# Interleaving the last sixteen adaLN modulation blocks with the first mixer tile

## The chip, the cores and the metric

The kernel runs on all 8 cores of one Trainium2 chip. Each core computes one element of the batch (4096 rows of 1024) with the same program; nothing is exchanged. The metric is the device time in microseconds of the slowest core.

## The reference

A hybrid decoder layer: adaLN modulation from a conditioning vector, a mixer (chunked gMLP gating beside multi-scale pooling), and a squared-ReLU MLP.

```python
mod = jax.nn.silu(c) @ w_ada + b_ada            # 1024 -> 6144, one row per core
shift1, scale1, gate1, shift2, scale2, gate2 = [
    m[:, None, :] for m in jnp.split(mod, N_MOD, axis=-1)]
h = rms_norm(x, norm1_pre) * (1.0 + scale1) + shift1
z = h @ w_in
y_a = spatial_gating(z[..., : 2 * D_A], ...)    # gelu, layer norm, 128x128 mixing
y_b = multiscale_pool(z[..., 2 * D_A:], ...)    # windows 2, 4, 8, 16
mix = jnp.concatenate([y_a, y_b], axis=-1) @ w_out
x = x + gate1 * rms_norm(mix, norm1_post)
h = rms_norm(x, norm2_pre) * (1.0 + scale2) + shift2
f = jnp.square(jax.nn.relu(h @ w_fc1)) @ w_fc2  # 1024 -> 4096 -> 1024
x = x + gate2 * rms_norm(f, norm2_post)
```

## The kernel before

The rows are worked in 16 tiles of 256. Weights w_in, w_out and w_fc1 stay in SBUF as bf16; their loads are issued on POOL's queue because they cast from float32 ("casts" below: w_out one of 4 MB read, w_fc1 four of 4 MB read). w_fc2 streams through three slab slots; in ffn(0) each slab is cast by a POOL DMA and written back to HBM by SP, later tiles read that copy.

Every engine runs its instructions in the order in which the program records them (`sc.op`, `sc.dma`); semaphore waits follow from the buffers named as read and written. A buffer that is overwritten waits for its readers.

*Modulation (L233 to L288).* w_ada is taken in 24 blocks of 256 columns, 1 MB each. A block b goes: SP loads it into staging slot b % 3 of `xb` (L237, needs the slot's last reader, L257, done) and a bias row into `rl` (L239, needs the matmul of block b-2 done). ScalarE multiplies by silu(c) in eight instructions (L250). VectorE adds up in three (L253, L255, L257), TensorE sums over the partitions (L261, L262, which also mark `modgate b`), VectorE copies the row out (L265). Then either TensorE turns the row into columns of PSUM bank 0 (L285; chunks 0, 1, 3, 4, here "plain" blocks), or, for the gates gate1 (blocks 8 to 11) and gate2 (blocks 20 to 23), TensorE broadcasts it (L273) and VectorE multiplies it into gp1 or gp2 (L276; here "gate" blocks). L298 to L302 then make the scale columns.

*Large weights.* POOL issues the cast of w_out after `modgate8` (L289), those of w_fc1 after `modgate12`, 16, 20 and 23 (L293). Every fc1 matmul (L616) names all four w_fc1 buffers as read.

*mixer(i)* is a generator. Between its yields stand these steps: norm_A (squares on ScalarE, then a chain of eight small VectorE instructions, L178 to L190); an empty one; norm_A2 (L346, L348); norm_B (transposes L359, scaling L368 on ScalarE and L377 on VectorE); z (L407, L412); u and v with pooling 0 and 1 and the layer norm (L450 to L487); pooling 2 and 3 (L426, L430); the spatial matmuls (L501, L509, L514); the pooling matmuls (L525, L534); the first and the second half of the output matmuls with the residual (L548 to L567), a step each; an empty one; norm_A, norm_A2, norm_B of the second norm. Tile 0's input sits in slot 0 of `xb`, which is also a staging slot.

*ffn(i)* runs fc1 and fc2 (L616, L635) over 16 pairs of hidden blocks; from its second step on it takes one step of mixer(i+1) after each of its own. mixer(0) has no ffn to stand beside and runs alone after block 23 (L686).

Of the kernel before, what the change touches and what calls it, by code (L numbers as in the profile page):

```python
# [78 lines left out]
def build(NT=16):  # L79
# [21 lines left out]
    sc = Sched()  # L101
# [3 lines left out]
    with contextlib.ExitStack() as _st:  # L105
# [32 lines left out]
        def buf(name):  # L138
            if name not in B:
                B[name] = Buf(name)  # L140
            return B[name]
# [88 lines left out]

        wada_v = wada_d.rearrange("p (b k c) -> p b k c", b=24, k=8)
        CH_COL = {0: 0, 1: 8, 3: 16, 4: 24}
        for b in range(24):  # L233
            st = b % 3
            stg = xb[:, st, :].rearrange("p (k c) -> p k c", c=256)
            stg_bufs = [buf("xb%d_0" % st), buf("xb%d_1" % st)]
            sc.dma(SP, lambda e, b=b, stg=stg: e.dma_start(out=stg, in_=wada_v[:, b, :, :]),  # L237
                   "wa%d" % (b % 3), writes=stg_bufs)
            sc.dma(SP, lambda e, b=b: e.dma_start(out=rl[0:1, b % 2, 0:256], in_=bada_d[0:1, b * 256:(b + 1) * 256]),  # L239
                   "ba%d" % (b % 2), writes=[buf("rl%d" % (b % 2))])  # L240
            pr = 4 + b % 2
# [13 lines left out]
            sc.op(DVE, lambda e, stg=stg: e.tensor_tensor(out=stg[:, 0:2, :], in0=stg[:, 0:2, :], in1=stg[:, 2:4, :],  # L255
                                                          op=ALU.add), reads=stg_bufs, writes=stg_bufs)
            sc.op(DVE, lambda e, stg=stg, accv=accv: e.tensor_tensor(out=accv, in0=stg[:, 0, :], in1=stg[:, 1, :],  # L257
                                                                     op=ALU.add), reads=stg_bufs, writes=[mb_])

            def mm_mod(e, b=b, pr=pr, accv=accv):  # L260
                e.matmul(ps[0:1, pr, 0:256], lhsT=ones[:, 0:1], rhs=accv, start=True, stop=False)  # L261
                return e.matmul(ps[0:1, pr, 0:256], lhsT=ones[0:1, 0:1], rhs=rl[0:1, b % 2, 0:256], start=False, stop=True)  # L262
            sc.op(PE, mm_mod, reads=[buf("macc%d" % (b % 2)), buf("ones"), buf("rl%d" % (b % 2))],
                  writes=[Bps(pr), buf("modgate%d" % b)])
            sc.op(DVE, lambda e, b=b, pr=pr: e.tensor_copy(out=tmp[0:1, b % 2, 0:256], in_=ps[0:1, pr, 0:256]),  # L265
                  reads=[Bps(pr)], writes=[buf("tmp%d" % (b % 2))])
            chunk = b // 4
            if chunk in (2, 5):
                gp = gp1 if chunk == 2 else gp2
                gpb = buf("gp1") if chunk == 2 else buf("gp2")  # L270
                pb = 6 + b % 2
                cols = slice((b % 4) * 256, (b % 4) * 256 + 256)
                sc.op(PE, lambda e, b=b, pb=pb: e.matmul(ps[:, pb, 0:256], lhsT=ones[0:1, :], rhs=tmp[0:1, b % 2, 0:256],  # L273
                                                        start=True, stop=True),
                      reads=[buf("tmp%d" % (b % 2)), buf("ones")], writes=[Bps(pb)])
                sc.op(DVE, lambda e, gp=gp, pb=pb, cols=cols: e.tensor_tensor(out=gp[:, cols], in0=ps[:, pb, 0:256],  # L276
                                                                          in1=gp[:, cols], op=ALU.mult),
                      reads=[Bps(pb), gpb], writes=[gpb])
            else:
                col0 = CH_COL[chunk] + (b % 4) * 2  # L280

                def mm_col(e, b=b, col0=col0):
                    ins = None
                    for q in range(2):
                        ins = e.matmul(ps[:, 0, col0 + q:col0 + q + 1], lhsT=tmp[0:1, b % 2, q * 128:(q + 1) * 128],  # L285
                                       rhs=ones[0:1, 0:1], start=True, stop=True)
                    return ins
                sc.op(PE, mm_col, reads=[buf("tmp%d" % (b % 2)), buf("ones")], writes=[Bps(0)])  # L288
        sc.dma(POOL, lambda e: e.dma_start(out=w_out_sb[:], in_=wout_d.rearrange("p (k n) -> p k n", k=8)),  # L289
               "w_out", reads=[buf("modgate8")], writes=[buf("w_out")])  # L290
        fc1_v = fc1_d.rearrange("p (k n) -> p k n", k=8)
        for q in range(4):
            sc.dma(POOL, lambda e, q=q: e.dma_start(out=fc1_sb[:, 2 * q:2 * q + 2, :], in_=fc1_v[:, 2 * q:2 * q + 2, :]),  # L293
                   "fc1_%d" % q, reads=[buf("modgate%d" % (12 + 4 * q if q < 3 else 23))], writes=[buf("fc1_%d" % q)])
        FC1 = [buf("fc1_%d" % q) for q in range(4)]

        x_load(0)
        sc.op(DVE, lambda e: e.tensor_copy(out=mc[:, 0:32], in_=ps[:, 0, 0:32]), reads=[Bps(0)], writes=[buf("mc_raw")])  # L298
        sc.op(DVE, lambda e: e.scalar_tensor_tensor(out=mc[:, 32:40], in0=mc[:, 8:16], scalar=1.0,
                                                    in1=cv[:, C_N1:C_N1 + 8], op0=ALU.add, op1=ALU.mult),  # L300
              reads=[buf("mc_raw"), buf("cv")], writes=[buf("mc_g1")])
        sc.op(DVE, lambda e: e.scalar_tensor_tensor(out=mc[:, 40:48], in0=mc[:, 24:32], scalar=1.0,  # L302
                                                    in1=cv[:, C_N2:C_N2 + 8], op0=ALU.add, op1=ALU.mult),
              reads=[buf("mc_raw"), buf("cv")], writes=[buf("mc_g2")])
        MODB = [buf("mc_raw"), buf("mc_g1"), buf("mc_g2")]
        G1, SH1, G2, SH2 = 32, 0, 40, 16

        sc.op(DVE, lambda e: e.tensor_tensor(out=vg[:, 0, :], in0=vg[:, 0, :], in1=vg[:, 1, :], op=ALU.mult),
# [40 lines left out]
                                                 op0=ALU.mult),  # L349
                  reads=[buf("xb%d_1" % slot), r_buf], writes=[buf("hbf_1")])  # L350

        def norm_B(dstT, dstT_buf, gcol, shcol):
            for s in range(2):
                mb = MB[s]

# [28 lines left out]
        def mixer(i):  # L384
# [6 lines left out]
            yield  # L391
            norm_A2(slot, r1, br1)
            yield
            norm_B(hT, "hP%d" % (i % 2), G1, SH1)
            yield
            if i > 0:
                sc.op(DVE, lambda e: e.tensor_copy(out=Z[:, :, 0:16], in_=Z[:, :, 256:272]),
# [176 lines left out]
            yield  # L574
            norm_A2(slot, r2, br2)
            yield
            norm_B(hT, "hP%d" % (i % 2), G2, SH2)
            yield

        def slab_load(G):  # L580
# [100 lines left out]
            yield  # L681

        stores = []
        if NT > 1:
            x_load(1)
        for _ in mixer(0):  # L686
            pass
        for i in range(NT):
            gm = mixer(i + 1) if i + 1 < NT else None
            step = 0  # L690
# [109 lines left out]
```

How the kernel before makes its waits and increments, by code:

```python
            def run(eng_name, eng):  # L715
                waited = {}
                for (deps, fn, key, amt) in sc.ops[eng_name]:
                    for (k_, v_) in deps:
                        if waited.get(k_, 0) >= v_:
                            continue
                        eng.wait_ge(sems[k_], v_)
                        waited[k_] = v_
                    if fn is None:
                        continue
                    ins = fn(eng)
                    ins.then_inc(sems[key], amt)
```

## Time and profile before

| | us |
|---|---|
| median of two runs | 1629.02 (1625.27 to 1632.77) |
| profiled execution, its own time | 1626.7 |
| its span, slowest core (core 4) | 1624.9 |
| spans of the eight cores | 1608.6 to 1624.9 |
| mean granted TensorE clock, die 0 and die 1 | 0.961, 0.958 |

All rows are of core 4. Times are microseconds from the start of the span. A timeline row reads: start, duration, engine, line, operation, output<-input with sizes, count of instructions merged, and in brackets the engine's idle time ahead of it and what ended it. PE is TensorE, DVE VectorE, ACT ScalarE, SPq the sequencer of SyncE that issues DMAs. A windows row gives a stretch, its length, for each engine the busy time and number of instructions (PE, PE's weight loads, DVE, ACT, POOL), the granted TensorE clock as a share of full speed, the mean busy share of the 16 DMA engines, and GB/s.

### The profile page before, as it was taken

To read this page: it belongs to the slowest core of one execution; us is meant where nothing else is said; L and a number is where in the kernel's file an instruction comes from. 1 tells how busy PE (TensorE), PEld (TensorE's weight loads), DVE (VectorE), ACT (ScalarE), POOL (GpSimd) and SP (SyncE) were. 2 spreads that over 40 slices of the span, in tenths; PEclk is the share of its full clock that TensorE was granted. 3 is DMA by queue.
4 is the path that set the end of the run, shared out by engine and by line. 5 is a ranking of instruction groups with operands and counts; after the bars stand their busy time and mean duration, and the time that the engine had idled before them with its cause. 6 is when DMAs were issued, how large, how long until landed. Compare 5 with 4: busy or idle time off the path is not lost.

```text
span 1624.9 us, 27071 instructions; the slowest of 8 cores (1608.6 to 1624.9 us)
## 1 busy us (share of the span) xinstructions
PE 1331.5 (82%) x8674; PEld 855.0 (53%) x8818; DVE 767.3 (47%) x1993; ACT 595.6 (37%) x1315; POOL 326.2 (20%) x319
## 2 busy tenths in 40 slices
PE   0543345989898989898989898989899898999896
PEld 0211023647565656565656565656566565656564
DVE  0443344445555454554546364645454545464531
ACT  1544323334342524242525242434343342424231
POOL 0000001322222122221222122222122222122221
PEclk9999987999999999999999999999999999999998
DMA  8478823994342424242524233343433342433243
GB/s 205 181 201 196 225 51 79 207 188 145 104 146 94 156 92 169 78 169 78 182 74 150 102 121 127 104 156 104 156 103 138 107 140 99 157 100 135 91 157 117
DMA packets 88491, 218.79 MB, mean 135 GB/s; under 512 B 5768, under 2 KB 5920, under 8 KB 84384
## 3 DMA queue, kind: packets, MB, share of 16 engines
q1 hardware_dynamic: 82704, 194.87, 35.0%
q0 software_dynamic: 5648, 22.19, 8.7%
q8 instruction: 73, 1.20, 0.3%
q14 instruction: 66, 0.54, 0.1%
HBM read 214.05 MB, written 25.17 MB: 147 GB/s over the span
## 4 chain that ended last, share of the span: by engine, by line
PE 54%; DVE 23%; DMA 11%; issue 6%; ACT 3%; POOL 1%; DVEq 1%; SPq 1%; ACTq 0%; POOLq 0%
PE ps L635 18%; PE ps L616 15%; PE ps L548 7%; DMA fc2buf<-fc2s 5%; DMA xb<-wada 5%; DVE pt L426 4%; PE ps L407 4%; PE ps L450 3%; PE ps L465 3%; DVE xb L673 3%; DVE tmpS L509 2%; DVE sm L187 2%; DVE xb L253 1%; DVE tmp L661 1%; DVE vg L661 1%
## 5 line engine op out<-in xcount | busy, mean ns | idle before, releaser
L616 PE MATMUL ps<-hP,fc_sb 128*128 128x256 bf16 x4096 | 510.4, 281 | 7.2 <-ACT rl L620 4.4
L635 PE MATMUL ps<-fc2buf,hid 128*128 128x512 bf16 x1936 | 474.7, 385 | 29.3 <-DMA fc2buf<-fc2s 13.8
L616 PEld LDWEIGHTS ps<-hP,fc_sb 128*128 128x128 bf16 x4096 | 410.2, 101 | 103.1 <-issue 11.7
L622 POOL TENSOR_TENSOR hid<-rl 128x512 bf16<-128x512 f32 x256 | 272.7, 1067 | 936.2 <-ACT rl L620 872.4
L635 PEld LDWEIGHTS ps<-fc2buf,hid 128*128 128x128 bf16 x2048 | 201.5, 100 | 226.3 <-issue 42.0
L620 ACT ACTIVATE rl<-ps 128x512 f32<-128x512 f32 x256 | 152.1, 595 | 421.1 <-PE ps L616 413.6
L261 PE MATMUL ps<-rl,ones_sb 128*1 128x256 f32 x48 | 24.3, 609 | 114.7 <-DVE rl L257 112.7
L548 PE MATMUL ps<-w_out_sb,yT 128*128 128x512 bf16 x496 | 116.4, 383 | 2.3 <-DVE yT L534 1.4
L250 ACT ACTIVATE xb<-xb,sm 128x256 f32<-128x256 f32 x192 | 78.4, 493 | 106.8 <-DMA xb<-wada 106.8
L368 ACT ACTIVATE hP<-ps,mc 128x128 bf16<-128x128 bf16 x256 | 92.7, 467 | 29.8 <-PE ps L359 29.8
L377 DVE TENSOR_SCALAR hP<-ps,mc 128x128 bf16<-128x128 bf16 x256 | 67.5, 337 | 73.5 <-PE ps L359 73.5
L552 ACT ACTIVATE junk<-ps 128x512 bf16<-128x512 f32 x64 | 38.2, 597 | 147.6 <-PE ps L548 143.3
L548 PEld LDWEIGHTS ps<-w_out_sb,yT 128*128 128x128 bf16 x512 | 50.3, 99 | 63.4 <-issue 4.6
L558 DVE TENSOR_TENSOR tmp<-ps,gp 128x512 f32<-128x512 f32 x32 | 22.1, 692 | 126.0 <-ACT junk L552 126.0
L426 DVE TENSOR_TENSOR pt<-Z 128x271 f32<-128x271 f32 x64 | 28.2, 440 | 106.8 <-ACT Z L412 103.3
L346 ACT ACTIVATE hbf<-xb,sm 128x1024 bf16<-128x1024 f32 x32 | 36.7, 1148 | 96.1 <-DVE sm L190 96.1
L340 ACT ACTIVATE junk<-xb 128x1024 bf16<-128x1024 f32 x64 | 67.4, 1053 | 8.3 <-DVE xb L567 5.2
L525 PE MATMUL ps<-diff,wpool_sb 128*128 128x256 bf16 x64 | 14.6, 317 | 65.9 <-DVE tmpS L509 65.9
L261 PEld LDWEIGHTS ps<-rl,ones_sb 128*1 128x1 f32 x48 | 2.7, 80 | 120.4 <-issue 120.4
L514 POOL TENSOR_TENSOR yT<-tmpS,ubf 128x512 bf16<-128x512 f32 x32 | 36.9, 1152 | 139.2 <-DVE tmpS L509 139.2
L187 DVE SCALAR_TENSOR_TENSOR sm<-sm 128x2 f32<-128x2 f32 (+1 forms) x192 | 54.8, 285 | 20.7 <-DVE sm L185 0.3
L661 DVE TENSOR_TENSOR tmp<-ps,gp 128x512 f32<-128x512 f32 x32 | 22.1, 692 | 89.5 <-ACT junk L655 88.1
(80 smaller groups left out, 1238.3 us busy)
## 6 DMA issues: line engine op xcount, KB each, us to landing
fc2buf<-fc2s SPq DMA_DIRECT2D x240, 512.0 KB, 3.8
xb<-wada SPq DMA_DIRECT2D x24, 1024.0 KB, 7.7
xb<-x SPq DMA_DIRECT2D x16, 1024.0 KB, 6.1
out<-xb SPq DMA_DIRECT2D x16, 1024.0 KB, 5.0
fc_sb<-w_fc POOLq DMA_DIRECT2D x4, 2048.0 KB, 19.9
fc2buf<-w_fc POOLq DMA_DIRECT2D x16, 512.0 KB, 7.8
fc2s<-fc2buf SPq DMA_DIRECT2D x16, 512.0 KB, 6.3
w_in_sb<-w_in POOLq DMA_DIRECT2D x2, 1536.0 KB, 23.4
```

What stands on the lines that cost most here:

```text
L187: sc.op(DVE, lambda e: e.scalar_tensor_tensor(out=u, in0=t, scalar=-0.5, in1=vv, op0=ALU.mult, op1=ALU.mult), reads=[bt_, bv], writes=[bu])
L250: ins = e.activation(out=stg[:, k, :], in_=stg[:, k, :], func=AF.Identity, scale=scv[:, k:k + 1])
L340: sc.op(ACT, lambda e, s=s: e.activation(out=junk[:], in_=xs(slot, s), func=AF.Square, accum_out=sm[:, ss_col + s:ss_col + s + 1]), reads= ...
L368: ins = e.activation(out=dstT[:, k, s * 128:(s + 1) * 128], in_=bank_bf(mb)[:, k * 128:(k + 1) * 128], func=AF.Identity, scale=mc[:, gcol ...
L377: ins = e.tensor_scalar(out=dstT[:, k, s * 128:(s + 1) * 128], in0=bank_bf(mb)[:, k * 128:(k + 1) * 128], scalar1=mc[:, gcol + k:gcol + k ...
L407: ins = e.matmul(ps[:, mb, gg * T:(gg + 1) * T], lhsT=w_in_sb[:, k, 1024 + g * 128:1024 + (g + 1) * 128], rhs=hT[:, k, :], start=(k == 0), ...
L426: sc.op(DVE, lambda e, src=src, dst=dst, lo=lo, sh=sh: e.tensor_tensor(out=dst[:, lo:272], in0=src[:, lo:272], in1=src[:, lo - sh:272 - sh ...
L548: ins = e.matmul(ps[:, mb, :], lhsT=yT[:, k, s * 128:(s + 1) * 128], rhs=w_out_sb[:, k, hf * 512:(hf + 1) * 512], start=(k == 0), stop=(k ...
L616: ins = e.matmul(ps[:, fb, jj * T:(jj + 1) * T], lhsT=fc1_sb[:, k, j * 128:(j + 1) * 128], rhs=h2T[:, k, :], start=(k == 0), stop=(k == 7))
L620: sc.op(ACT, lambda e: e.activation(out=rl[:, jp % 2, :], in_=ps[:, fb, :], func=AF.Relu), reads=[Bps(fb)], writes=[buf("rl%d" % (jp % 2))])
L622: sc.op(POOL, lambda e: e.tensor_tensor(out=hid[:, jp % 3, :], in0=rl[:, jp % 2, :], in1=rl[:, jp % 2, :], op=ALU.mult), reads=[buf("rl%d" ...
L635: ins = e.matmul(ps[:, 2 * s + hf, :], lhsT=hid[:, jp % 3, jj * T + s * 128:jj * T + (s + 1) * 128], rhs=fc2buf[:, sl, jj, hf * 512:(hf + ...
```

## The change

The modulation block becomes a function `mod_block(b)`. Blocks 0 to 7 run as before on three staging slots. Then the scale and shift of the first norm are made (`mod_cols(1)`), tile 0 is loaded into slot 0 and mixer(0) is begun: after each of the blocks 8 to 23 the generator takes one step. These blocks have two staging slots, 1 and 2. The gate broadcast moves from PSUM banks 6 and 7, which the mixer uses, to 2 and 3. The columns of the second norm are made after block 19. The large casts are issued behind the blocks that gate them (`late_weights`), since POOL's queue now also holds instructions of mixer(0). L308 to L318 (the spatial weights) now stand ahead of block 0 instead of behind block 23.

```diff
-        for b in range(24):
-            st = b % 3
+        def mod_block(b):
+            st = b % 3 if b < 8 else 1 + b % 2
...
-                   "wa%d" % (b % 3), writes=stg_bufs)
+                   "wa%d" % st, writes=stg_bufs)
...
-                pb = 6 + b % 2
+                pb = 2 + b % 2
...
+        def late_weights(b):
+            if b == 8:
+                sc.dma(POOL, lambda e: e.dma_start(out=w_out_sb[:], in_=wout_d.rearrange("p (k n) -> p k n", k=8)),
+                       "w_out", reads=[buf("modgate8")], writes=[buf("w_out")])
+            for q in range(4):
+                if b == (12 + 4 * q if q < 3 else 23):
+                    sc.dma(POOL, lambda e, q=q: e.dma_start(out=fc1_sb[:, 2 * q:2 * q + 2, :],
+                                                            in_=fc1_v[:, 2 * q:2 * q + 2, :]),
+                           "fc1_%d" % q, reads=[buf("modgate%d" % b)], writes=[buf("fc1_%d" % q)])
+
+        def mod_cols(which):
+            lo = 0 if which == 1 else 16
+            sc.op(DVE, lambda e: e.tensor_copy(out=mc[:, lo:lo + 16], in_=ps[:, 0, lo:lo + 16]),
+                  reads=[Bps(0)], writes=[buf("mc_raw%d" % which)])
...
-        if NT > 1:
-            x_load(1)
-        for _ in mixer(0):
-            pass
+        for b in range(8):
+            mod_block(b)
+        mod_cols(1)
+        x_load(0)
+        gm0 = mixer(0)
+        for b in range(8, 24):
+            mod_block(b)
+            late_weights(b)
+            if b == 19:
+                mod_cols(2)
+            try:
+                next(gm0)
+            except StopIteration:
+                pass
+        for _ in gm0:
+            pass
+        if NT > 1:
+            x_load(1)
```

## Rows read from the trace of the kernel before

**Rows 1.** The page, busy time of each engine.
```profile
PE 1331.5 (82%) x8674; PEld 855.0 (53%) x8818; DVE 767.3 (47%) x1993; ACT 595.6 (37%) x1315; POOL 326.2 (20%) x319
```

**Rows 2.** Windows view: modulation, mixer(0), its last part, ffn(0).
```profile
0.00:203.50 203.50, 71.94 (x176) 23.40 (x176) 68.01 (x107) 79.90 (x194) 5.47 (x15) 1.00 0.77 202
203.50:271.30 67.80, 29.91 (x156) 17.07 (x159) 32.30 (x115) 21.16 (x47) 4.44 (x5) 0.78 0.36 76
...
246.00:271.30 25.30, 10.45 (x47) 4.83 (x49) 12.43 (x43) 9.09 (x21) 1.29 (x2) 0.70 0.58 125
...
271.30:362.60 91.30, 81.19 (x531) 53.31 (x541) 35.01 (x100) 29.63 (x62) 28.73 (x31) 0.93 0.79 164
```

**Rows 3.** Timeline from 75 to 87 us: a plain block, then a gate block.
```profile
75.01 1.20 DVE L253 TENSOR_TENSOR xb<-xb 128x1024 f32<-128x1024 f32 x1
75.47 3.30 ACT L250 ACTIVATE xb<-xb,sm 128x256 f32<-128x256 f32 x8 [2.33 <-DMA xb<-wada]
...
77.11 0.42 DVE L257 TENSOR_TENSOR rl<-xb 128x256 f32<-128x256 f32 x1
...
79.84 0.41 DVE L265 COPY tmp<-ps 1x256 f32<-1x256 f32 x1 [2.30 <-PE ps L262]
80.18 1.20 DVE L253 TENSOR_TENSOR xb<-xb 128x1024 f32<-128x1024 f32 x1
...
85.46 0.53 POOL L289 DMA_DIRECT2D w_out_sb<-w_out  x1 [81.52 <-PE ps L262]
...
86.94 0.42 DVE L276 TENSOR_TENSOR gp<-ps,gp 128x256 f32<-128x256 f32 x1 [1.51 <-PE ps L273]
```

**Rows 4.** Timeline: a w_ada load, a wait for a load, the last fc1 cast.
```profile
92.93 0.33 SPq L237 DMA_DIRECT2D xb<-wada  x1
...
144.17 1.23 DVE L253 TENSOR_TENSOR xb<-xb 128x1024 f32<-128x1024 f32 x1 [11.06 <-ACT xb L250]
...
201.65 0.53 POOL L293 DMA_DIRECT2D fc_sb<-w_fc  x1 [20.66 <-PE ps L262]
```

**Rows 5.** DMA issues (43.5, 92.9, 85.5, 201.7): KB written, us to landing.
```profile
xb<-wada SPq DMA_DIRECT2D x1, 1024.0 KB, 5.6
...
xb<-wada SPq DMA_DIRECT2D x1, 1024.0 KB, 15.5
...
w_out_sb<-w_out POOLq DMA_DIRECT2D x1, 2048.0 KB, 22.0
...
fc_sb<-w_fc POOLq DMA_DIRECT2D x1, 2048.0 KB, 14.6
```

**Rows 6.** Timelines of ACT, PE and DVE: mixer(0) and ffn(0)'s start and end.
```profile
210.17 0.75 DVE L348 TENSOR_SCALAR hbf<-xb,sm 128x1024 bf16<-128x1024 f32 x1
...
212.66 2.90 ACT L368 ACTIVATE hP<-ps,mc 128x128 bf16<-128x128 bf16 x8 [1.36 <-PE ps L359]
...
216.02 6.38 PE L407 MATMUL ps<-hP,w_in_sb 128*128 128x256 bf16 x32 [2.60 <-DVE hP L377]
222.24 3.66 PE L450 MATMUL ps<-hP,w_in_sb 128*128 128x256 bf16 x32
...
233.59 1.00 DVE L487 TENSOR_SCALAR vn<-vg,sm 128x512 bf16<-128x512 f32 x2
...
240.07 1.13 DVE L509 SCALAR_TENSOR_TENSOR tmpS<-ps,cv,Bt 128x128 f32<-128x128 f32 x4
...
243.76 1.93 DVE L534 TENSOR_SCALAR yT<-ps,cv 128x256 bf16<-128x256 f32 x4
...
245.94 8.75 PE L548 MATMUL ps<-w_out_sb,yT 128*128 128x512 bf16 x31 [1.36 <-DVE yT L534]
...
256.50 1.28 DVE L558 TENSOR_TENSOR vg<-ps,gp 128x512 f32<-128x512 f32 x2
...
271.33 7.79 PE L616 MATMUL ps<-hP,fc_sb 128*128 128x256 bf16 x48 [2.81 <-DVE hP L377]
...
359.28 3.57 PE L635 MATMUL ps<-fc2buf,hid 128*128 128x512 bf16 x8 [5.25 <-DMA fc2buf<-w_fc]
```

More of the change, by code:

```diff
@@ L288, in build @@
                 sc.op(PE, mm_col, reads=[buf("tmp%d" % (b % 2)), buf("ones")], writes=[Bps(0)])
-        sc.dma(POOL, lambda e: e.dma_start(out=w_out_sb[:], in_=wout_d.rearrange("p (k n) -> p k n", k=8)),
-               "w_out", reads=[buf("modgate8")], writes=[buf("w_out")])
         fc1_v = fc1_d.rearrange("p (k n) -> p k n", k=8)
-        for q in range(4):
-            sc.dma(POOL, lambda e, q=q: e.dma_start(out=fc1_sb[:, 2 * q:2 * q + 2, :], in_=fc1_v[:, 2 * q:2 * q + 2, :]),
-                   "fc1_%d" % q, reads=[buf("modgate%d" % (12 + 4 * q if q < 3 else 23))], writes=[buf("fc1_%d" % q)])
@@ L295, in build @@
         FC1 = [buf("fc1_%d" % q) for q in range(4)]
[L297 to L304, printed above, removed]
@@ L305, in build @@
-        MODB = [buf("mc_raw"), buf("mc_g1"), buf("mc_g2")]
+        def late_weights(b):
[7 more added lines that the diff above has]
+                           "fc1_%d" % q, reads=[buf("modgate%d" % b)], writes=[buf("fc1_%d" % q)])
@@ new lines, in mod_cols @@
+        def mod_cols(which):
+            lo = 0 if which == 1 else 16
+            sc.op(DVE, lambda e: e.tensor_copy(out=mc[:, lo:lo + 16], in_=ps[:, 0, lo:lo + 16]),
+                  reads=[Bps(0)], writes=[buf("mc_raw%d" % which)])
+            gcol = 32 if which == 1 else 40
+            ncol = C_N1 if which == 1 else C_N2
+            sc.op(DVE, lambda e: e.scalar_tensor_tensor(out=mc[:, gcol:gcol + 8], in0=mc[:, lo + 8:lo + 16], scalar=1.0,
+                                                        in1=cv[:, ncol:ncol + 8], op0=ALU.add, op1=ALU.mult),
+                  reads=[buf("mc_raw%d" % which), buf("cv")], writes=[buf("mc_g%d" % which)])
@@ L306, in build @@
+        MODB1 = [buf("mc_raw1"), buf("mc_g1")]
+        MODB2 = [buf("mc_raw2"), buf("mc_g2")]
         G1, SH1, G2, SH2 = 32, 0, 40, 16
@@ L350, in norm_A2, with norm_B @@
                   reads=[buf("xb%d_1" % slot), r_buf], writes=[buf("hbf_1")])
-        def norm_B(dstT, dstT_buf, gcol, shcol):
+        def norm_B(dstT, dstT_buf, gcol, shcol, MODB):
             for s in range(2):
@@ L393, in mixer @@
             yield
-            norm_B(hT, "hP%d" % (i % 2), G1, SH1)
+            norm_B(hT, "hP%d" % (i % 2), G1, SH1, MODB1)
             yield
@@ L576, in mixer @@
             yield
-            norm_B(hT, "hP%d" % (i % 2), G2, SH2)
+            norm_B(hT, "hP%d" % (i % 2), G2, SH2, MODB2)
             yield
```

## Prediction

> **What bounds the kernel now.** I read the page first. TensorE is busy for 82% of the span [rows 1], so in the long run of 16 tiles only TensorE work counts. The slices show an exception at the left edge, so I cut the start into stretches [rows 2]: 203.5 us of modulation with TensorE busy for 72, then 67.8 us of mixer(0) alone (30 busy), then ffn(0), 91.3 us (81 busy). TensorE becomes the bound only at 271.3, where the first fc1 matmul starts [rows 6]. The question is how much earlier or later that matmul starts, and whether ffn(0) still takes 91 us.
>
> Within the modulation stretch I read the combined timeline for the period of a block [rows 3]. VectorE sets it. A plain block goes from one L253 (75.01) to the next (80.18), 5.2 us; a gate block (chunks 2 and 5) from 80.18 to the end of L276 at 87.3, 7.1 us (7.05 from start to start). Most of that is not work: L265 waits 2.30 us for L261/L262 and L276 waits 1.51 us for L273, and VectorE's queue is in order, so nothing fills these waits. ScalarE's eight products (3.30 us) run ahead of VectorE and are hidden. Blocks 8 to 23 are 8 plain and 8 gate blocks, 8 x 5.2 + 8 x 7.05 = 98 us; they occupy 80.2 to 203.5, 123 us, so 25 us are waits for loads. The longest, 11.06 us [rows 4], falls while an fc1 cast is under way.
>
> **The loads.** A w_ada load alone lands in 5.6 us. The one issued at 92.93, some 7 us after w_out (85.46), took 15.5 us, until w_out's 22.0 us were over [rows 3 to 5]. So a load issued late in a cast's shadow lands when the cast does, plus about 1 us. The last fc1 cast, with little beside it, took 14.6 us from 201.65 [rows 4, 5].
> The Trainium skill (DMA: Bandwidth & Descriptors, Queues, rings and completion order) says a DMA engine takes the queues that have work in turn, packet by packet; by that a load of 5.6 us would need about 11 us beside a cast, and the trace's 15.5 is longer, so I keep the row. By the rule block 11 below comes some 4 us earlier and the result would be 1651 instead of 1655.
>
> **The change part by part.** I write S for the start of L253 of a block. From S: L257 is done at 2.6, modgate at 5.3, the block ends at 5.2 (plain) or 7.05 (gate) [rows 3].
>
> *Blocks 0 to 7* keep three staging slots. The spatial-weight preparation (L308 to L318) now stands ahead of block 0, in time that the first load leaves idle: about 4 us leave the mixer's start. Block 7 stays at S = 75.0, and mod_cols(1) ends at 82.0 (end of block 80.3, a wait like L276's, two 0.2 us instructions).
>
> *Two slots from block 8 on.* Load 8 went out three blocks ahead; now it takes slot 1, which block 7 frees at 77.6. It lands at 83.2, the products end at 86.6, S8 = 86.7, against 80.2 before: 6.5 us late (1.8 for mod_cols(1), 4.7 of wait for the load). From here load b+2 waits for L257 of block b, where before load b+3 did: two loads ahead instead of three. In SP's queue ba(b) and the next load stand behind it, and x_load(0) waits for block 6 (5.2 us earlier, no delay).
>
> *One mixer step after each block.* Within each in-order queue a step's instructions now stand between two blocks: TensorE's behind the block's column or gate matmul, ScalarE's ahead of the next block's products, VectorE's ahead of its adds. Where a step ends on ScalarE, the next block's 3.3 us of products, hidden before, is exposed. The durations of the steps are those of before [rows 6].
> - b8, norm_A: the chain L178 to L190 ahead of L348 (210.17), eight instructions at 0.27 us, 2.1 us. S9 = 86.7+7.05+2.1 = 95.9.
> - b9, empty: S10 = 102.9. b10, norm_A2: 0.75. It would be 110.8, but load 11 (issued 98.5) is in the shadow of w_out, issued at S8+5.3 = 92.0 and landing at 114: it lands at 114.9, plus 3.3: S11 = 118.3 (7.5 us of wait).
> - b11, norm_B: its transposes start at about 124.7, ScalarE's eight copies (2.90, begun 1.1 behind) end at 128.6, block 12's products at 131.9: S12 = 132.0 (6.6 over the block).
> - b12, z: TensorE 138.3 to 144.7 (32 matmuls, 6.4 us), copy to 145.4, products to 148.7: S13 = 148.8 (11.6).
> - b13, u and v: start 155.2. Before it was 12.3 us from the start of u (222.24) to the end of L487 (234.6), with ScalarE done early enough for the products to fit; I add 1.8 because u restarts at the slow rate (32 matmuls took 6.38 us in z, 3.66 in u): S14 = 169.4 (15.4).
> - b14, pooling 2 and 3: 234.5 to 240.07, 5.6. S15 = 180.2.
> - b15, mm_s: L509 twice (1.13), POOL's product between, and their waits, up to L534 at 243.76: 3.8, plus 1.9 for the matmul that used to run ahead. S16 = 191.1. b16, mm_p: 4.0. S17 = 200.3.
> - b17, b18, mm_o: 245.94 to 256.50 was 10.6 from the first matmul to the end of the first half; each half now starts behind the column matmul, 12.1 over the block. S18 = 217.6, S19 = 234.9.
> - b19, mod_cols(2): 1.8. S20 = 241.9. b20, norm_A: 2.1. S21 = 251.0. b21: 0.8. S22 = 258.9.
> - b22, norm_B: as b11. Load 23 is issued at 253.7 in the shadow of fc1_2 (issued 247.2), lands 266 to 270. S23 = 272.6.
>
> In sum from the end of block 7: 80.3 + blocks 98 + steps 85.6 + load waits 12.2 + columns 3.5 = 279.6. The loads' old waits (25 us) are nearly all taken up by mixer steps: that is the gain. Against it stand the exposed products and the loss of mixer(0)'s own overlap between steps. Modulation plus mixer ends about 279.7 against 271.3.
>
> *The last fc1 cast.* late_weights(23) is gated on modgate23 as before, but before its 14.6 us ran under mixer(0) (201.65 to about 216, wanted at 271.3). Now modgate23 comes at 277.9 with the mixer already done, and L616 reads all four fc1 buffers: the cast's cover is gone. 277.9+14.6+0.3 = 292.8. Delay so far 292.8-271.3 = **21.5 us**. Bounds: 14.6 to 22.0 (w_out, same size, with loads beside it) for the cast, so 21.5 to 29.
>
> *ffn(0).* The casts of slabs 0 to 2 with their write-backs ran ahead of fc1. They now queue on POOL behind the last fc1 cast. Slab 0 is wanted 7.8 us after the first fc1 matmul (48 matmuls in 7.79 us) and lands about 5.6 us after it, if its 1 MB takes what a w_ada load takes: no stall there. But ffn(0) already has 72 us of DMA work in 91.3 (share 0.79) and ended on a 5.25 us wait for a slab [rows 2, 6]. The slabs' work ahead of fc1 was 0.58 of 25.3 us, 15 us [rows 2]; with it ffn(0) has 87 of 91. Between nothing and 15 I take **5**, since the fill is just under the stretch. x_load(1) goes out when block 22 frees slot 1 (261.5) and is wanted only in ffn(0): nothing. Banks 2 and 3 instead of 6 and 7 for the gates: nothing, they are idle until ffn(0).
>
> Sum: +21.5 +5 = +26.5 on the profiled run's 1626.7 = 1653.2. The two timed runs' median is 1629.0, 2.3 above; against that I predict **1655**, 1.6% slower.
>
> **The rivals.**
> 1. *The interleave works as meant.* If steps ran in the load waits and in VectorE's 2.3 us waits, block 23 would end near 203.5+12 and only the cast would follow: 271.3 becomes about 230, 41 us less, 1588 (faster by 2.5%). For it: 25 us of load wait, and VectorE is idle for 35 of mixer(0)'s 68 us [rows 2]. Against it: a queue in order can't place a step into a wait inside a block. It decides for faster once 60 of the steps' 85 us cost nothing (26.5 to regain, 33 to win). 5%.
> 2. *Steps overlap more than reckoned.* If the products run in time (the 3.3 us at b11, b12, b17, b18, b22 hidden) and loads share fairly, 16 to 20 us go: 1637. 20%.
> 3. *DMA fills ffn(0).* The 15 us of slab work come in full and the last cast takes 22: +10 and +7.4, 1672, slower by over 2%. For it: the share above and the wait at 359. 25%.
> 4. *TensorE stays slow.* If u, v and mm_o all run at z's rate (32 + 2 x 16 + 2 x 32 = 128 matmuls' worth of 256 columns, 0.085 us more for each), another 11 us: 1666. For it: the granted clock of the mixer stretch was 0.78, in bursts far less broken up than the new ones [rows 2]. 10%.
> The Trainium skill (TensorE: Matmul & The Clock Gate, What's actually happening) has the array at 1.2 GHz until it has been busy; z against u agrees, and this is the rule that speaks for rival 4.
>
> **How the numbers follow.** Forecast (1645 to 1662) 40%. The range 1632 to 1676 holds it, rivals 2 and 3 and most of 4. A measurement of this kernel tells about 2%: the bounds are 1596 and 1662. Faster: rival 1, 5%. Slower: rival 3, half of rival 4 and a few per cent of the forecast's upper edge, 32%. Within: 63%.
>
> **What would show it.** L253 of block 23 near 272 and no load wait over 8 us; VectorE's waits for ScalarE (L250) at blocks 12, 13 and 23; the wait of L616 for the fc1 cast, about 15 us, ahead of the first fc1 matmul at 293; ffn(0) 91 to 100 us; from there on the old rate. It is wrong if the first fc1 matmul starts before 280 (steps overlap) or if ffn(0) exceeds 105 us.

## The result and the profile after

The changed kernel takes 1652.1 us against 1628.2 of before. The ratio is 1.0155 (95% interval 1.0134 to 1.0175): slower by 1.55%, some 25 us. The prediction said 1655. A few executions of any kernel fall into a slower state, in which half of the cores show a lower granted clock; the medians below are of all executions, the ratios leave those out.

The profiled execution has a span of 1650.3 us, 25.4 more than before. Where it lies is read from the windows view of the changed kernel (columns as in [rows 2]): blocks 0 to 7 with the first columns; blocks 8 to 23 with mixer(0); the wait for the last w_fc1 cast; ffn(0); the rest.

```profile
0.00:82.00 82.00, 25.49 (x66) 9.45 (x66) 23.89 (x41) 28.40 (x67) 2.82 (x10) 1.00 0.69 190
82.00:276.50 194.50, 79.93 (x264) 32.85 (x266) 77.39 (x180) 71.95 (x174) 5.40 (x7) 0.70 0.52 130
276.50:293.40 16.90, 1.19 (x2) 0.50 (x2) 0.42 (x1) 0.00 (x0) 2.58 (x4) 0.50 0.86 138
293.40:385.20 91.80, 81.24 (x531) 53.00 (x541) 35.01 (x100) 29.66 (x62) 28.78 (x31) 0.93 0.89 195
385.20:1650.30 1265.10, 1152.68 (x7812) 762.64 (x7943) 631.52 (x1672) 465.54 (x1012) 287.16 (x268) 0.96 0.37 125
```

The first fc1 matmul starts at 293.4 instead of 271.3 [rows 6], which is 22.1 of the 25.4 us. ffn(0) takes 91.8 instead of 91.3 [rows 2], the remaining fifteen tiles 1265.1 instead of 1262.3. So the change lost its time ahead of ffn(0), as a wait in which hardly anything but the DMA engines is at work (the third line, 16.9 us) and as a merged stretch that is longer than the two it was made of (194.5 us against the 191.1 from 80.2 to 271.3 before).

The second, the longer merged stretch, shows in VectorE's waits, blocks 8 to 23 of the changed kernel (engine and line waiting, what for, us in total, times, the longest):

```profile
DVE tmp L265 <- PE ps L262: 37.0, 16, 2.3
DVE xb L253 <- ACT xb L250: 28.5, 5, 11.3
DVE gp L276 <- PE ps L273: 10.2, 7, 1.5
DVE sm L483 <- ACT vg L477: 8.5, 1, 8.5
DVE tmp L566 <- ACT junk L560: 7.4, 2, 5.6
DVE vg L566 <- ACT junk L560: 6.9, 2, 5.7
```

Sixteen times 2.3 us for L262: the wait inside each block is just what it was [rows 3], although ready mixer work now stands in the same queue, behind it. The timeline of ScalarE shows the other half of the matter, at blocks 12 and 13:

```profile
123.47 2.91 ACT L376 ACTIVATE hP<-ps,mc 128x128 bf16<-128x128 bf16 x8 [7.77 <-PE ps L367]
126.23 3.31 ACT L250 ACTIVATE xb<-xb,sm 128x256 f32<-128x256 f32 x8
139.73 0.60 ACT L420 ACTIVATE Z<-ps 128x512 f32<-128x512 f32 x1 [10.19 <-PE ps L415]
142.33 0.60 ACT L420 ACTIVATE Z<-ps 128x512 f32<-128x512 f32 x1 [2.01 <-PE ps L415]
142.83 3.28 ACT L250 ACTIVATE xb<-xb,sm 128x256 f32<-128x256 f32 x8
```

ScalarE stands idle for 7.8 and 10.2 us for the step's matmuls, although the next block's load has landed (block 12's at 114.7, block 13's at 123.9); its products come after.

### The profile page after: what moved, and what is told of

Its sections match the earlier page's. It is cut to its first block, busy times and chain, and to the rows that moved or that the text cites. A ratio compares the mean times of both kernels' runs of the same rounds, so it can differ in the third digit from the quotient of the medians.

```text
span 1650.3 us, 27057 instructions; the slowest of 8 cores (1632.7 to 1650.3 us)
## 1 busy us (share of the span) xinstructions
PE 1340.5 (81%) x8674; PEld 858.4 (52%) x8818; DVE 768.2 (47%) x1994; ACT 595.5 (36%) x1315; POOL 326.7 (20%) x319
## 4 chain that ended last, share of the span: by engine, by line
PE 55%; DVE 21%; DMA 11%; issue 6%; ACT 4%; POOL 1%; DVEq 1%; SPq 1%; ACTq 0%; POOLq 0%
PE ps L643 18%; PE ps L624 15%; PE ps L556 7%; DMA fc2buf<-fc2s 6%; DVE pt L434 4%; PE ps L458 4%; PE ps L415 4%; PE ps L473 3%; DMA xb<-wada 3%; DVE xb L681 3%; DVE tmpS L517 2%; DVE sm L187 2%; DVE xb L253 2%; PE ps L261 1%; PE ps L262 1%
## 5 line engine op out<-in xcount | busy, mean ns | idle before, releaser
L624 PE MATMUL ps<-hP,fc_sb 128*128 128x256 bf16 x4096 | 512.9, 282 | 20.4 <-DMA fc_sb<-w_fc 15.7
L643 PE MATMUL ps<-fc2buf,hid 128*128 128x512 bf16 x1936 | 475.8, 385 | 28.4 <-DMA fc2buf<-fc2s 12.6
L261 PE MATMUL ps<-rl,ones_sb 128*1 128x256 f32 x48 | 24.3, 608 | 124.7 <-DVE rl L257 124.7
L376 ACT ACTIVATE hP<-ps,mc 128x128 bf16<-128x128 bf16 x256 | 92.9, 468 | 47.2 <-PE ps L367 47.2
L566 DVE TENSOR_TENSOR tmp<-ps,gp 128x512 f32<-128x512 f32 x32 | 22.1, 692 | 129.7 <-ACT junk L560 129.7
L669 DVE TENSOR_TENSOR tmp<-ps,gp 128x512 f32<-128x512 f32 x32 | 22.1, 692 | 93.3 <-ACT junk L663 92.0
L187 DVE SCALAR_TENSOR_TENSOR sm<-sm 128x2 f32<-128x2 f32 (+1 forms) x192 | 55.3, 288 | 21.8 <-DVE sm L185 1.7
L190 DVE SCALAR_TENSOR_TENSOR sm<-sm 128x2 f32<-128x2 f32 (+1 forms) x192 | 53.6, 279 | 21.1 <-DVE sm L187 0.9
## 6 DMA issues: line engine op xcount, KB each, us to landing
fc_sb<-w_fc POOLq DMA_DIRECT2D x4, 2048.0 KB, 17.4
```

Source lines behind the costliest of these rows:

```text
L187: sc.op(DVE, lambda e: e.scalar_tensor_tensor(out=u, in0=t, scalar=-0.5, in1=vv, op0=ALU.mult, op1=ALU.mult), reads=[bt_, bv], writes=[bu])
L376: ins = e.activation(out=dstT[:, k, s * 128:(s + 1) * 128], in_=bank_bf(mb)[:, k * 128:(k + 1) * 128], func=AF.Identity, scale=mc[:, gcol ...
L624: ins = e.matmul(ps[:, fb, jj * T:(jj + 1) * T], lhsT=fc1_sb[:, k, j * 128:(j + 1) * 128], rhs=h2T[:, k, :], start=(k == 0), stop=(k == 7))
L643: ins = e.matmul(ps[:, 2 * s + hf, :], lhsT=hid[:, jp % 3, jj * T + s * 128:jj * T + (s + 1) * 128], rhs=fc2buf[:, sl, jj, hf * 512:(hf + ...
```

## The experiments

"First fc1" is the start of the first fc1 matmul in the profiled execution, on the core with the longest span, from which all rows are read; the column beside it is its mean over the eight cores of that execution. Ratios are to the kernel before, with 95% intervals.

| kernel | first fc1, us | mean of 8 cores | median, us | ratio |
|---|---|---|---|---|
| before | 271.3 | 266.5 | 1628.2 | 1 |
| changed | 293.4 | 289.0 | 1652.1 | 1.0155 (1.0134 to 1.0175) |
| changed, casts early | 277.9 | 275.2 | 1640.1 | 1.0079 (1.0048 to 1.0111) |
| changed, products ahead | 278.2 | 273.7 | 1638.1 | 1.0053 (1.0028 to 1.0078) |
| changed, third slot | 285.4 | 283.3 | 1649.5 | 1.0106 (1.0068 to 1.0145) |
| changed, tails later | 277.4 | 272.7 | 1638.0 | 1.0052 (1.0035 to 1.0069) |
| changed, third slot and casts early | 272.2 | 269.6 | 1635.2 | 1.0051 (1.0030 to 1.0072) |
| changed, products ahead and tails later | 263.3 | 259.1 | 1623.0 | 0.9961 (0.9944 to 0.9977) |
| changed, all four | 241.9 | 236.9 | 1599.6 | 0.9810 (0.9787 to 0.9833) |
| all four, gates later too | 247.9 | 239.1 | 1598.9 | 0.980 (0.974 to 0.986) |
| before, two slots | 295.6 | 290.1 | 1653.0 | 1.0122 (1.0074 to 1.0169) |
| before, slabs late | 272.5 | 267.5 | 1638.2 | 1.0049 (1.0026 to 1.0072) |
| before, tails later | 275.0 | 262.3 | 1629.3 | 0.9992 (0.9970 to 1.0013) |
| before, tails later, x first | 263.5 | 257.1 | 1619.8 | 0.9945 (0.9925 to 0.9966) |

Within one execution the cores start fc1 at times far apart (259.4 to 272.4 in the kernel before, 281.8 to 293.4 in the changed one), and the slowest core is not the same one in each kernel. So a difference of 2 or 3 us in the first column alone says nothing.

### The last cast, given back its cover

```diff
-                if b == (12 + 4 * q if q < 3 else 23):
+                if b == 11 + 3 * q:
```

> The changed kernel with one edit: the four w_fc1 casts go out behind blocks 11, 14, 17 and 20 instead of 12, 16, 20 and 23. My theory: the last cast lost its cover, and its 15.7 us wait ahead of the first fc1 matmul is pure loss. Then the wait is gone, the first fc1 matmul starts at about 279 instead of 293.4, and the time is about 1638 (14.5 us less than the changed kernel, still 0.6% over before). Rival: the start is bound by the bytes to move, so that casts issued earlier only hold up the w_ada loads by as much; then the wait before fc1 goes, but L253 of block 23 comes some 10 to 15 us later and the time stays near 1652.

The chain of the changed kernel in order of time (start, length, what) has the cast as a link of its own. In the edited kernel's timeline the last cast goes out at 245.4 and the first fc1 matmul waits for nothing:

```profile
276.43 16.88 DMA fc_sb<-w_fc
293.44 7.72 PE ps L624 x48
```

```profile
245.35 0.53 POOL L298 DMA_DIRECT2D fc_sb<-w_fc  x1 [41.29 <-PE ps L262]
...
277.93 6.73 PE L624 MATMUL ps<-hP,fc_sb 128*128 128x256 bf16 x48
```

15.5 us went from the first fc1 matmul (13.8 in the mean of the cores), and block 23's adds stood at 271.4 against 271.1: moving the casts cost the loads nothing. The theory holds, the rival falls. The time fell by 12 us. On this core, the slowest, the fc2 matmuls of the later tiles waited 22.1 us for their slabs against 12.6 on the changed kernel's slowest; on four other cores of this execution the same waits come to 10.8 to 17.9 us (more on this under ffn(0) below).

### The next block's products ahead of the step

mod_block is taken apart: mod_head is the load, the bias row and ScalarE's products, mod_adds is L253 to L262, mod_tail is L265 and the columns or the gate.

```diff
+        mod_head(8)
         for b in range(8, 24):
-            mod_block(b)
+            mod_adds(b)
+            mod_tail(b)
             late_weights(b)
+            if b < 23:
+                mod_head(b + 1)
...
                 next(gm0)
```

> The changed kernel with one edit: from block 8 on the load and ScalarE's eight products of block b+1 are recorded ahead of the mixer step that follows block b, so they no longer stand behind the step's ScalarE instructions. My theory: the step's order exposes 3.3 us of products at blocks 12, 13 and 23 (VectorE waited 3.2, 11.3 and 3.2 us for L250 there); the edit gives back about 9.5 us, the first fc1 matmul starts at about 284, time about 1643. Rival: the loads are the limit, the products end when they did, and nothing changes (1652).

The start moved by 15.2 us, not 9.5. The row of the waits that answers to the 28.5 us above is, in this kernel:

```profile
DVE xb L255 <- ACT xb L246: 13.1, 3, 6.3
```

28.5 - 13.1 = 15.4 is the gain (15.3 in the mean of the cores). I had counted 3.3 us of exposed products at each of three blocks; at block 13 more than the products could go, since its wait of 11.3 us also held z's matmuls and copies, on which the block's products and adds don't depend.

### A third staging slot

```diff
-            st = b % 3 if b < 8 else 1 + b % 2
-            stg = xb[:, st, :].rearrange("p (k c) -> p k c", c=256)
+            st = b % 3 if b < 8 else (3, 2, 1)[(b - 8) % 3]
+            if st == 3:
+                stg = fc2buf[:].rearrange("p a j n -> p (a j n)").bitcast(F32)[:, 0:2048].rearrange(
+                    "p (k c) -> p k c", c=256)
+                stg_bufs = [buf("f2b0"), buf("f2b1")]
```

> The changed kernel with one edit: blocks 8 to 23 have a third staging slot again, in the memory of the first two w_fc2 slabs, which is idle until then. My theory: two slots cost the waits at block 8 (6.2 us before its adds, of which some 5 go) and block 11 (4.6 us), and little elsewhere, because mixer steps take up the other load waits: 8 us less, time about 1644, first fc1 matmul at about 285. Rival: the two slots are the main reason that block and step times add up, and a third gives back over 20 us (under 1632).

8.0 us at the first fc1 matmul, as expected, though 5.7 in the mean of the cores. Of that 2.7 show in the medians, and the ratio fell by 0.5% with intervals that overlap: the fifteen tiles behind ffn(0) took 1274.7 us here instead of 1265.1. The time alone would not have settled it.

### Two slots where nothing is interleaved

```diff
-            st = b % 3
+            st = b % 3 if b < 8 else 1 + b % 2
```

> The kernel before with one edit: two staging slots from block 8 on (1 and 2 in turn), nothing interleaved. My theory: here no mixer step covers a load wait, so two slots cost more than in the changed kernel: load 5.6 + products 3.3 + adds 2.6 + gaps make 11.7 us for two blocks' slots, 5.9 a block instead of 5.2 for 8 plain blocks (+5), block 8's own wait (+5) and longer waits behind the casts (up to 10): 1638 to 1648. Rival: the staging depth matters as little as in the changed kernel's blocks 12 to 23: under 1633.

The first fc1 matmul moved by 24.3 us (23.6 in the mean), more than I expected. VectorE waited for products 48.6 us in eight blocks, where before it waited 24.7 in three. Three of the eight, blocks 8, 11 and 15:

```profile
87.77 1.23 DVE L253 TENSOR_TENSOR xb<-xb 128x1024 f32<-128x1024 f32 x1 [8.13 <-ACT xb L250]
116.61 1.23 DVE L253 TENSOR_TENSOR xb<-xb 128x1024 f32<-128x1024 f32 x1 [7.55 <-ACT xb L250]
152.80 1.23 DVE L253 TENSOR_TENSOR xb<-xb 128x1024 f32<-128x1024 f32 x1 [11.22 <-ACT xb L250]
```

The same two slots cost 24 us here and 8 in the changed kernel. That is what the interleave gives: mixer steps take up two thirds of such load waits or more (23.6 against 5.7 us in the means).

### The block's tail one block later

```diff
         for b in range(8, 24):
-            mod_block(b)
+            mod_head(b)
+            mod_adds(b)
+            mod_tail(b - 1)
...
+        mod_tail(23)
```

> The changed kernel with one edit: what follows the partition sums of a block (the copy L265 and the columns or the gate) is recorded behind the adds of the next block, so VectorE no longer stands still 2.3 us (plain) or 3.8 us (gate) in each block. My theory: the in-order waits inside the blocks are what keeps the interleave from filling anything; without them up to 8 x 2.3 + 8 x 3.8 = 49 us could go from blocks 8 to 23, of which other waits (products behind a step's ScalarE work, loads behind casts) take back perhaps half: first fc1 matmul at 262 to 272, time about 1625. Rival: the loads become the bound at once and under 10 us go (1642 or more).

The edit does the same in blocks 0 to 7 and moves the norm columns one block later. 16.0 us (16.3 in the mean), of at most 49: between the theory (21 to 31) and the rival (under 10). About 4 of them were won before the interleaved part: block 8's adds begin at 83.3 instead of 87.2. The waits of VectorE in this kernel say where the rest went:

```profile
DVE xb L255 <- ACT xb L246: 33.2, 5, 9.4
DVE gp L281 <- PE ps L278: 23.6, 8, 3.2
DVE sm L488 <- ACT vg L482: 10.3, 1, 10.3
```

The 37.0 us for L262 are gone. But the gate's broadcast now stands in TensorE's queue behind the next block's sums, so its wait went from 1.5 to up to 3.2 us each, and the products are waited for 33.2 us instead of 28.5: one in-order wait handed part of its time to the next.

### Both edits of order

```diff
+        mod_head(8)
         for b in range(8, 24):
-            mod_block(b)
+            mod_adds(b)
+            mod_tail(b - 1)
             late_weights(b)
+            if b < 23:
+                mod_head(b + 1)
```

> The changed kernel with the two edits of order together: the tails one block later and the load and products of the next block ahead of the mixer step; two slots and the late casts stay. Alone they moved the first fc1 matmul by 15.2 and 16.0 us. With the tails alone VectorE then waited 33 us for ScalarE's products, which is what the other edit takes away, so my theory is that they add up at least: first fc1 matmul at 262 or earlier, time about 1621 or less. Rival: both take away the same idle time, first fc1 matmul not before 270, time 1630 or more.

```profile
DVE xb L255 <- ACT xb L246: 16.9, 2, 9.8
```

30.1 us together against 15.2 and 16.0 alone (in the means 29.9 against 15.3 and 16.3): they add up, and the wait for products is 16.9 instead of 33.2 us. With two slots and the late cast (its wait is still 14.0 us) this kernel is already faster than before.

### Third slot and early casts, order unchanged

```diff
-            st = b % 3 if b < 8 else 1 + b % 2
+            st = b % 3 if b < 8 else (3, 2, 1)[(b - 8) % 3]
...
-                if b == (12 + 4 * q if q < 3 else 23):
+                if b == 11 + 3 * q:
```

> The changed kernel with two of the edits together: the third staging slot and the w_fc1 casts behind blocks 11, 14, 17 and 20; the order of block and mixer step is left as it is. My theory: the two costs that the change brought along (8.0 us for the slots, 15.5 for the cast) are separate and make up the whole loss, and the interleave in itself gains nothing. Then the first fc1 matmul starts at 293.4 - 8.0 - 15.5 = 270 and the time is that of before within 0.3% (1624 to 1633). Rival: they overlap (the earlier casts hold up loads that a third slot would have brought in time), 1636 or more; or the interleave has a gain of its own that shows now, under 1620.

The first fc1 matmul starts at 272.2, 0.9 us from that of before, and 3.1 later in the mean of the cores: the two costs are separate (19.4 us together in the mean, 13.8 and 5.7 alone), and with both taken away the interleave in its original order gains nothing at this point. The time missed my band: 1.0051 is 8 us, not under 5. On the core of these rows ffn(0) ends at 360.8, 1.8 us earlier than before, and the other fifteen tiles take 1277 us instead of 1262.3. TensorE's waits for slabs in them come to 17.4 us instead of 13.8, and the fc2 group right after such a wait runs slow:

```profile
1580.98 3.57 PE L648 MATMUL ps<-fc2buf,hid 128*128 128x512 bf16 x8 [3.50 <-DMA fc2buf<-fc2s]
```

That makes some of the 15 us; why these waits differ I can't tell. Two of the eight cores have such a long rest, and this execution took 1639.8 us against the median of 1635.2, so the 15 us are not the kernel's.

### All four

```diff
-            st = b % 3 if b < 8 else 1 + b % 2
+            st = b % 3 if b < 8 else (3, 2, 1)[(b - 8) % 3]
...
-                if b == (12 + 4 * q if q < 3 else 23):
+                if b == 11 + 3 * q:
...
+        mod_head(8)
         for b in range(8, 24):
-            mod_block(b)
+            mod_adds(b)
+            mod_tail(b - 1)
             late_weights(b)
+            if b < 23:
+                mod_head(b + 1)
```

> The changed kernel with the four edits together: tails one block later, products of the next block ahead of the step, a third staging slot, w_fc1 casts behind blocks 11, 14, 17 and 20. If each lever is independent, 25 + 9 + 8 + 15 us go: first fc1 matmul at about 235, time about 1594, 2% faster than before. The bound below is the DMA work of the start, 0.77 of 203.5 us = 157 us plus x and the slabs: not under 195 for the first fc1 matmul. Rival: loads and casts then collide and most of the gain over the tails alone is lost (over 1610).

```profile
0.00:78.00 78.00, 24.19 (x62) 8.51 (x62) 23.16 (x38) 28.40 (x67) 2.83 (x10) 1.00 0.76 201
78.00:241.90 163.90, 78.39 (x272) 32.54 (x272) 76.51 (x183) 71.60 (x174) 7.98 (x10) 0.72 0.66 170
241.90:336.40 94.50, 82.78 (x541) 53.34 (x541) 36.19 (x101) 29.67 (x62) 28.57 (x31) 0.92 0.84 188
```

15.5 + 15.2 + 8.0 + 16.0 = 54.7 us alone, 51.5 together (in the means 51.1 and 52.1), and the time is 28.6 us under before. It beats both kernels. The stretch from 78 to 241.9 does the work that took 191.1 us from 80.2 to 271.3 before.

### The gates one block later as well

mod_gate is VectorE's multiplication with the broadcast gate (L276), taken out of mod_tail.

```diff
+            mod_gate(b - 2)
             mod_tail(b - 1)
-            if b == 8:
+            if b == 9:
                 mod_cols(1)
```

> The kernel with the four edits (1599.6 us, first fc1 matmul at 241.9) with one more edit of the same kind: VectorE's multiplication of a gate block (after the gate broadcast) and the two sets of norm columns are recorded one block later. There VectorE waited 22.1 us in seven gate blocks for the broadcast and 5.9 us for the columns. My theory: VectorE's in-order waits are still what spaces the blocks, and 15 to 25 us go: first fc1 matmul at 220 to 227, time about 1582. Rival: the casts' shadow over the loads is the limit by now (DMA share 0.66 over the stretch, one wait of 9.9 us for a load), and under 8 us go (1592 or more).

The rival was right. VectorE's 23.6 us for the broadcast in eight blocks fell to 3.2, 2.9 of it at block 23, and the time stayed. In the waits of VectorE, then of ScalarE, of this kernel:

```profile
DVE xb L258 <- ACT xb L249: 21.9, 3, 12.2
DVE fc2buf L258 <- ACT fc2buf L249: 13.9, 3, 9.1
```

```profile
ACT xb L249 <- DMA xb<-wada: 40.4, 4, 19.3
ACT fc2buf L249 <- DMA fc2buf<-wada: 31.7, 4, 10.3
```

VectorE waits 35.8 us for products instead of 11.1, and ScalarE 72.1 us for loads instead of 62.6. The time that this edit freed went to waits for loads. Whether another order would give more was not tried.

### Tails later without any interleave

```diff
+        for b in range(24):
+            mod_block(b)
+            if b > 0:
+                mod_tail(b - 1)
+        mod_tail(23)
```

mod_block is here the loop's body of the kernel before, up to L262.

> The kernel before with one edit: the tails one block later, no interleave. My theory: without VectorE's waits a block needs 2.6 + 0.4 us of VectorE and 3.3 of ScalarE, so the loads set the pace; the modulation ends at about 180 instead of 203.5 (DMA work 157 us of it), 20 to 25 us less: about 1606. Rival: the three slots keep only three loads in flight and the casts hold them up as before, so under 10 us go (1619 or more).

Block 23's adds began 9.7 us earlier (186.7 against 196.4) and the time did not move, as the rival had it, though for another reason: the first fc1 matmul came at 275.0. The gain was handed to the load of x tile 0:

```profile
209.04 1.06 ACT L349 ACTIVATE junk<-xb 128x1024 bf16<-128x1024 f32 x1 [11.83 <-DMA xb<-x]
...
xb<-x SPq DMA_DIRECT2D x1, 1024.0 KB, 29.8
```

x tile 0 went out at 179.2, behind one cast (176.0, 20.3 us), and before it was done the next went out (192.0, 18.1 us). Cores 3 and 6 show the same wait (9.2 and 10.5 us); the other cores don't, and the mean start is 4.2 us earlier than before. The slowest core sets the time.

### The same, with x tile 0 ahead of the last cast

```diff
-                   "fc1_%d" % q, reads=[buf("modgate%d" % (12 + 4 * q if q < 3 else 23))], writes=[buf("fc1_%d" % q)])
+                   "fc1_%d" % q, reads=[buf("modgate%d" % (12 + 4 * q if q < 3 else 23))] + (
+                       [buf("xb0_0")] if q == 3 else []), writes=[buf("fc1_%d" % q)])
```

> The kernel before with the tails one block later, as in the run that gained nothing, and in addition the last w_fc1 cast held until x tile 0 has landed. There block 23's adds began 10 us earlier than before, but ScalarE then waited 11.8 us for x tile 0, which was issued at 179 and landed at 209 behind two casts. My theory: the time was not lost in the order but handed to that load; with only one cast ahead of it x lands at about 198, the first fc1 matmul starts at about 264 and the time is about 1618. Rival: the x tile is held up by the loads' own traffic just as long, or the last cast now comes too late for fc1, and the time stays at 1626 to 1630.

```profile
197.60 0.53 POOL L303 DMA_DIRECT2D fc_sb<-w_fc  x1 [21.50 <-DMA xb<-x]
```

The tile landed at 197 after 18.4 us, the first fc1 matmul started at 263.5, the time is 1619.8. All three numbers as expected: a dependency that held back one cast by 5.6 us (197.6 against 192.0) bought 11.5 us on the slowest core, 5.2 in the mean. It is also the measure for the kernel with all four edits: 8 of its 28.6 us under before can be had with no interleave at all; no run without one reaches the other 20.

### The slabs of w_fc2 late

```diff
                 fc1(jp)
+                if i == 0 and jp == 0:
+                    slab_load(0)
+                    slab_load(1)
+                    slab_load(2)
```

> The kernel before with one edit: the casts of w_fc2 slabs 0 to 2 are issued by POOL only behind the first fc1 pair of ffn(0), not during mixer(0). It tests the one term of my sum that the changed kernel's trace does not bear out: I put 5 us (0 to 15) for 15 us of slab work that falls into ffn(0), and ffn(0) took 91.8 us against 91.3. If DMA work of the slabs fills ffn(0), this kernel loses at least 5 us (1634 or more), and more than the changed kernel since the casts start even later. Rival: ffn(0) hides them except for the first slab's landing, which fc2(0) then waits for some 5 us at the start.

```profile
272.50:372.80 100.30, 82.18 (x531) 53.12 (x541) 34.31 (x100) 29.56 (x62) 31.04 (x34) 0.91 0.86 181
...
284.88 3.19 PE L630 MATMUL ps<-fc2buf,hid 128*128 128x512 bf16 x7 [5.64 <-DMA fc2buf<-w_fc]
```

The time is 10 us longer, as the theory wanted, but by the rival's mechanism. ffn(0) took 100.3 us instead of 91.3. Its DMA share, 0.86, is below the 0.89 that the changed kernel's ffn(0) reached in 91.8 us, so it isn't the DMA work that fills it. TensorE's waits for slabs in it come to 13.9 us in four places, 5.6 of them fc2(0)'s, against 5.9 in two before and 6.3 in three in the changed kernel. There the same casts went out 16 us ahead of the first fc1 matmul, while it waited for w_fc1, and cost nothing.

## Why the prediction was right, and where it was not

**The sum.** The starts of L253 (S) in the changed kernel, against the prediction's: block 8 at 87.2 (86.7), 11 at 115.8 (118.3), 13 at 146.2 (148.8), 14 at 167.6 (169.4), 17 at 198.4 (200.3), 19 at 233.6 (234.9), 23 at 271.1 (272.6); the first fc1 matmul at 293.4 (292.8). Two of the rows:

```profile
146.21 1.23 DVE L253 TENSOR_TENSOR xb<-xb 128x1024 f32<-128x1024 f32 x1 [11.29 <-ACT xb L250]
...
271.13 1.22 DVE L253 TENSOR_TENSOR xb<-xb 128x1024 f32<-128x1024 f32 x1 [3.19 <-ACT xb L250]
```

The waits for products came at blocks 12, 13 and 23, as named (3.2, 11.3 and 3.2 us). That the total came out within 3 us was luck in part: it rests on errors that cancel, 5 us put on ffn(0) against 0.5 measured, nothing put on the other tiles against 2.8, and a cast 2.3 us longer behind a block 23 that was 1.5 us early.

**The blocks' own waits stay.** Right, and the experiments show it from both sides: the interleave alone is worth nothing at the first fc1 matmul (272.2 against 271.3 with slots and cast mended), and the same steps with their neighbours reordered are worth 30 us, of which about 4 lie in blocks 0 to 7.

**The two slots.** The term (4.7 us at block 8, 7.5 at block 11) measured 6.2 and 4.6, 10.8 instead of 12.2, of which a third slot gave back 8.0. That the loads' old waits are taken up by steps was argued there and is shown now by 24 us against 8.

**Loads in a cast's shadow.** Load 11 went out at 98.97, w_out at 92.55. w_out landed after 18.5 us, at 111.1; the load after 13.3, at 112.3:

```profile
xb<-wada SPq DMA_DIRECT2D x1, 1024.0 KB, 13.3
```

The load landed with the cast, as reckoned; my cast of 22.0 us [rows 5] was 3.5 too long, which is the 2.5 us that S11 came early. The reason lies in the packets. Here is what the two queues moved between 97 and 105 us in the kernel before, with w_out's cast and the load of 92.93 under way (packets, MB, share of the 16 engines' time):

```profile
q0 software_dynamic: 63, 1.03, 78.3%
q1 hardware_dynamic: 64, 0.52, 20.5%
```

One packet of the load went for each of the cast, but a packet of the cast holds 16 KB written and took four times as much engine time as one of the load's 8 KB. The Trainium skill's rule (DMA: Bandwidth & Descriptors, Queues, rings and completion order), by which a DMA engine takes the queues in turn, packet by packet, is thus what the trace shows. What was wrong in the prediction is the 11 us drawn from it, which need turns of equal length. (Its sum by that rule was off as well: 98.5 + 11 + 3.3 is 5.5 us ahead of 118.3, not 4.)

**The cover of the last cast.** Right, and the largest single term: 15.7 us of wait by TensorE's row, 15.5 given back when the cast went out three blocks earlier. The cast took 16.9 us, not 14.6: the term was 2.3 short, made up for by S23 being 1.5 early.

**ffn(0).** This step failed. I put 5 us for slab work that moves into ffn(0); the changed kernel lost 0.5, with its DMA share up from 0.79 to 0.89. A share near one in the sum is not a delay as long as each slab comes before its matmul, and nearly all did, since the first ones went out during the wait. What costs is a slab that comes late at the start: 9 us in the kernel made for it.

In the other fifteen tiles, where I had nothing, 2.8 us came instead. On the slowest cores these tiles took 1253 to 1265 us in eleven of the fourteen profiled executions, and 1275 to 1277 in three (casts early, third slot, and the two together). The other cores say how much of that is the kernel's. From the first fc1 matmul to the end the eight cores need 1344 to 1356 us before (mean 1350.8) and 1347 to 1358 in the changed kernel (mean 1353.5). With the casts early they need 1348 to 1357 and one core 1366.3 (mean 1355.1); with both edits 1345 to 1356 and two cores 1365.7 (mean 1355.5). So there it is one or two cores of one execution. Only the third slot's mean, 1358.8, lies clearly higher; why stays open. The kernel with the slabs late has 1360.9, on all cores.

**TensorE at the slow rate.** This term was too small. z took 6.20 us, u 6.44 (3.66 before), v 3.40, the halves of mm_o 5.57 and 5.59, together 27.2 us against 22.2. u alone lost 2.8 us where I had put 1.8, and the step after block 13 took 16.2 us over the block instead of 15.4. The windows of z, u, v and the first half of mm_o:

```profile
135.98:142.18 6.20, 6.20 (x33) 4.34 (x32) 0.00 (x0) 0.60 (x1) 0.00 (x0) 1.00 1.12 210
152.55:158.99 6.44, 6.44 (x33) 4.64 (x34) 1.66 (x6) 0.60 (x1) 0.00 (x0) 0.56 0.16 66
159.04:162.44 3.40, 3.40 (x15) 1.37 (x14) 0.00 (x0) 2.01 (x5) 0.00 (x0) 1.00 0.00 0
205.09:210.66 5.57, 5.57 (x15) 1.96 (x14) 0.69 (x1) 0.69 (x2) 0.00 (x0) 0.61 0.89 199
```

u ran at a granted clock of 0.56 (mostly 1.2 GHz); from 142 to 152 us, ahead of it, TensorE had been busy for 2.5 of 10 us; v, right behind it, ran at full clock (2.4 GHz). The halves of mm_o had 0.61 and 0.64, against 0.83 in one piece before. Over the stretch the granted clock was 0.70, and 0.50 between 170 and 200 us, where TensorE was busy for 10.7 of 30 us. The Trainium skill's account (TensorE: Matmul & The Clock Gate, What's actually happening), slow until kept busy, agrees with these. For z only its duration does: the granted clock reads 1.00 there, in both kernels, so the trace doesn't show why z is slow. Rival 4 thus had 2.8 us in u and 2.4 in mm_o, some 5 of its 11.

**The rivals.** Rival 1 (faster by 2.5%) needed the steps to fall into the waits. In the kernel with all four edits they do, and the first fc1 matmul comes at 241.9, near the 230 that I had worked out for it, but the change as made leaves them where they were. Of rival 2's hidden products those behind b17 and b18 did run in time (VectorE waited for none at blocks 18 and 19), those at blocks 12 and 23 did not. Rival 3's filled ffn(0) did not come, and the last cast took 16.9 us, not 22.

## What to carry to other kernels

To interleave two stages in in-order queues is not to overlap them. In these runs it gained only where an instruction of the one stood ahead of a wait of the other in the same queue, so the parts to move are the waiting ones: what waits for another engine goes behind the next piece's ready work, what feeds the next piece goes ahead of the guest's work. Before a stage is hidden, list what it was hiding itself (here the last w_fc1 cast, and three slabs) and start that earlier.

## What the runs showed of the hardware

A 1 MB load of w_ada (5.6 us alone) issued 6 to 7 us into a 4 MB cast from the other queue landed about 1 us after the cast both times: 13.3 us in the changed kernel, 15.5 before. The queues alternated packet by packet, and a cast's packet (16 KB) took four times the engine time of a load's (8 KB). The x tile, 1 MB as well, goes in packets of 4 KB and so needs twice as many turns. These are the queues in the kernel before with tails later, from 184 to 192 us:

```profile
q0 software_dynamic: 76, 1.25, 96.5%
q1 hardware_dynamic: 73, 0.29, 11.2%
```

Issued 3 us into a cast, that tile took 29.8 us when a second cast went out before it had landed, and 18.4 once that cast was held back. What a load beside a cast waits for is its number of packets, more than its bytes. That fits all these rows, but no run changed the size of a packet.
